# Tables 4 to 7 of the S5 mixer asked for at once by ScalarE, in memory of their own

## What is computed

```python
def s5_layer(u, a_re, a_im, b_re, b_im, c_re, c_im, d_skip, log_dt, w_glu):
    A_bar = jnp.exp(dt * A)                        # 64 groups, 64 complex states each
    bu = jnp.einsum('blgk,gpk->blgp', ug, B_bar)
    _, states = lax.associative_scan(combine, (a, bu), axis=1)
    y = jnp.einsum('gkp,blgp->blgk', C_mat, states).real.reshape(Bsz, L, Dm)
    y = jax.nn.gelu(y + d_skip.astype(f32) * uf).astype(u.dtype)
    y1, y2 = jnp.split(y @ w_glu, 2, axis=-1)
    return y1 * jax.nn.sigmoid(y2)
```

## Time and profile before

| | |
|---|---|
| median of 3 runs | 2110.14 us (2110.12 to 2112.23) |
| profiled execution, its own time | 2109.24 us |
| its span | 2106.9 us (2.3 us lie around it) |
| PE busy | 2045.2 us, 97% of the span |
| DVE, ACT, POOL busy | 1155.7, 603.3, 46.2 us |
| S5 mixer, blocks 0 to 7 | from 1573 to about 1660 us |
| granted TensorE clock, mean | 0.992 of full |
| DMA | 314.90 MB, SyncE's queue (q1) 287.32, ScalarE's (q10) 26.48 |

### The profile page before, as it was taken

The page is one execution under the profiler, slowest core; times in us unless marked ns, Lnnn a source line. Parts: engine busy times, 40 slices in busy tenths (PEclk is TensorE's granted clock), DMA queues, the critical chain, the costliest instruction groups (busy, mean ns, idle before and its releaser), DMA issues.

```text
span 2106.9 us, 26044 instructions
## 1 busy us (share of the span) xinstructions
PE 2045.2 (97%) x10332; PEld 1744.3 (83%) x10332; DVE 1155.7 (55%) x1653; ACT 603.3 (29%) x717; POOL 46.2 (2%) x55
## 2 busy tenths in 40 slices
PE   4999999999999999999999999999998999999998
PEld 3788888998898889888888988888877798888886
DVE  6677556655455436887444566644458564333322
ACT  2322221423323223222222323322231333222222
POOL 2000000000000000000000000000002000000000
PEclk9999999999999999999999999999999999999999
DMA  8455555433233143667544254544766423233221
GB/s 319 144 195 192 187 190 175 141 120 105 75 109 105 65 155 116 200 229 232 183 166 150 94 159 148 169 148 149 243 206 232 158 80 100 100 100 100 90 95 55
DMA packets 246575, 314.90 MB, mean 149 GB/s; under 512 B 31904, under 2 KB 219552, under 8 KB 244128
## 3 DMA queue, kind: packets, MB, share of 16 engines
q1 hardware_dynamic: 214160, 287.32, 41.4%
q10 hardware_dynamic: 32336, 26.48, 3.8%
HBM read 290.44 MB, written 27.53 MB: 151 GB/s over the span
## 4 chain that ended last, share of the span: by engine, by line
PE 76%; issue 15%; DVE 4%; DMA 3%; ACT 1%; POOL 0%; SPq 0%; ACTq 0%; POOLq 0%; DVEq 0%
PE ps L1779 18%; PE ps L1780 18%; PE ps L1781 18%; PE ps L1806 7%; PE ps L1807 7%; PE ps L1810 7%; DMA y_dram<-s_buf 1%; DVE ada_first L972 1%; DMA y_dram<-acc 1%; PE ps L2058 1%; DMA sq<-y_dram 1%; DMA csil<-in_c 0%; DVE w_lo L962 0%; PE ps L1901 0%; PE ps L2049 0%
## 5 line engine op out<-in xcount | busy, mean ns | idle before, releaser
L557 ACT ACTIVATE w_hi<-w_raw 128x1024 fp32r<-128x1024 f32 x352 | 345.9, 1029 | 353.7 <-PE ps L1781 241.1
L962 DVE TENSOR_TENSOR w_lo<-w_raw,w_hi 128x1024 fp32r<-128x1024 f32 x172 | 210.2, 1222 | 371.8 <-ACT w_hi L557 369.9
L1779 PE MATMUL ps<-g_hi,w_lo 128*128 128x512 f32 (+1 forms) x952 | 345.7, 363 | 0.0
L1781 PE MATMUL ps<-g_hi,w_hi 128*128 128x512 f32 (+1 forms) x952 | 344.9, 362 | 0.0
L1780 PE MATMUL ps<-g_lo,w_hi 128*128 128x512 f32 (+1 forms) x952 | 344.9, 362 | 0.0
L1779 PE MATMUL ps<-h_hi,w_lo 128*128 128x512 f32 x880 | 344.2, 391 | 0.3 <-DVE w_lo L962 0.3
L1781 PE MATMUL ps<-h_hi,w_hi 128*128 128x512 f32 x880 | 342.7, 389 | 0.0
L1780 PE MATMUL ps<-h_lo,w_hi 128*128 128x512 f32 x880 | 342.6, 389 | 0.0
L1806 PE MATMUL ps<-h_hi,w_lo 128*128 128x512 f32 x688 | 269.8, 392 | 2.3 <-DVE w_lo L962 2.0
L1807 PE MATMUL ps<-h_hi,w_hi 128*128 128x512 f32 x688 | 268.6, 390 | 0.0
L1810 PE MATMUL ps<-h_lo,w_hi 128*128 128x512 f32 x688 | 212.3, 390 | 0.0
(11 more groups left out here) (264 smaller groups left out, 2314.1 us busy)
## 6 DMA issues: line engine op xcount, KB each, us to landing
w_raw<-in_ffn_w_in SPq DMA_DIRECT2D x86, 1024.0 KB, 6.6
ada_raw<-in_ada_w SPq DMA_DIRECT2D x128, 512.0 KB, 4.6
w_raw<-in_ffn_w_out SPq DMA_DIRECT2D x32, 1024.0 KB, 6.5
w_raw<-in_ret_w_in SPq DMA_DIRECT2D x24, 1024.0 KB, 5.3
w_raw<-in_ffn_w_out SPq DMA_DIRECT2D x16, 768.0 KB, 4.5
tb<-s_rec SPq DMA_DIRECT2D x6, 1536.0 KB, 6.7
w_raw<-in_ret_w_out SPq DMA_DIRECT2D x8, 1024.0 KB, 5.1
w_raw<-in_s_w_glu SPq DMA_DIRECT2D x8, 1024.0 KB, 6.1
```

What stands on the lines that cost most here:

```text
L557: copy = lambda o, i: nc.scalar.activation(o, i, ACT.Copy)
L962: V.tensor_tensor(w_lo[k % 2][:, 0:HALF, :], w_raw[k % 2][:, 0:HALF, :], raw_f32(w_hi[k % 2][:, 0:HALF, :]), ALU.subtract).then_inc(w_lo_h ...
L1779: nc.tensor.matmul(o, wl, xh, start=start, stop=False)
L1781: return nc.tensor.matmul(o, wh, xh, start=False, stop=stop)
```

## The change

- ScalarE asks for tables 4 to 7, all eight DMAs, directly behind `gelu(0)`, after a wait until the last part of GLU weight pair 0 has been split. They go on ScalarE's DMA queue. They are no longer issued by SyncE, whose waits for them in the loop are gone.
- Table 6 lies over `w_raw[0]` and `w_raw[1]`, table 7 over table 0. Tables 4 and 5 stay where they were.
- GLU pair 1 is loaded into `w2_raw`, over table 2, is asked for behind the read of hop 3, with no wait on `w_lo_done`, and its split parts lie over tables 1 and 3.
- GLU pair 2, which goes into `w_raw`, waits for `outputs(6)`.

```diff
+        w_raw_at = place["end"]
         w_raw = [sb(f"w_raw{s}", [P, 8, CW]) for s in range(2)]
...
-        tables = [*tb, tb[2], tb[3]]
-        w2_hi, w2_lo = ([sb(f"w2_{part}{k}", [P, 8, CW], F32R, h_at + HB * k + 4 * 8 * CW * (part == "lo")) for k in range(2)]
-                        for part in ("hi", "lo"))
+        tables = [*tb, sb("tb6", [P, REC], F32, w_raw_at), tb[0]]
+        w2_raw = [sb(f"w2_raw{k}", [P, 8, CW], F32, g_at + 4 * 8 * CW * k) for k in range(2)]
+        w2_hi, w2_lo = ([sb(f"w2_{part}{k}", [P, 8, CW], F32R, (h_at, g_at)[k] + HB + 4 * 8 * CW * (part == "lo"))
+                         for k in range(2)] for part in ("hi", "lo"))
...
                 def glu_pair(dp):
+                    if dp == 2:
+                        sp.wait_ge(y_done, 7)
...
-                    if b + 4 < KT:
-                        sp.wait_ge(yt_in[b % 2], 16 * (b // 2 + 1))
-                        if b >= 2:
-                            sp.wait_ge(y_done, b + 1)
-                        table(b + 4)
-                    if b == 4:
-                        glu_pair(1)
+                    if b == 3:
+                        for k in range(2):
+                            sp.dma_start(w2_raw[k][:], glu_w[:, :, CW + (D, 0)[k]:2 * CW + (D, 0)[k]]).then_inc(w_landed[k], 16)
...
-                    copy(w2_hi[k][:, 0:HALF, :], w_raw[k][:, 0:HALF, :]).then_inc(w_hi_half, 1)
-                    copy(w2_hi[k][:, HALF:8, :], w_raw[k][:, HALF:8, :]).then_inc(w_hi_done, 1)
+                    copy(w2_hi[k][:, 0:HALF, :], w2_raw[k][:, 0:HALF, :]).then_inc(w_hi_half, 1)
+                    copy(w2_hi[k][:, HALF:8, :], w2_raw[k][:, HALF:8, :]).then_inc(w_hi_done, 1)
...
                     A(gy[b % 2], ps[:, 4 + 2 * (b % 2)], ACT.Gelu_apprx_tanh).then_inc(gelu_done, 1)
+                    if b == 0:
+                        act.wait_ge(w_lo_done, C_GLU + 3)
+                        for later in range(4, KT):
+                            act.dma_start(tables[later][:, 0:R_MT], rec[later]).then_inc(tb_in[later], 16)
+                            act.dma_start(tables[later][:, R_MT:REC], lag_rec[later]).then_inc(tb_in[later], 16)
...
-                    V.tensor_tensor(w2_lo[k][:, r, :], w_raw[k][:, r, :], raw_f32(w2_hi[k][:, r, :]),
+                    V.tensor_tensor(w2_lo[k][:, r, :], w2_raw[k][:, r, :], raw_f32(w2_hi[k][:, r, :]),
```

## The result

| | before | after |
|---|---|---|
| median | 2110.01 us (2108.33 to 2112.23, 12 runs) | 2112.71 us (2110.07 to 2114.11, 12 runs) |
| ratio to before | | 1.0015, 95% interval 1.0008 to 1.0022 |
| profiled execution, its own time | 2109.24 us | 2113.4 us |
| its span | 2106.9 us | 2110.9 us |

What follows compares the result with a forecast made beforehand. TensorE bounds the kernel, with mixer waits on transfers worth at most 9.4 us. Scan 3, 11.9 us late, less 9.4 gives +2.5: 2111.7 against the profiled 2109.24, plus 0.9 for the median, 2112.6; 8-in-10 range 2102.5 to 2117.

Steps and rivals of the forecast that it cites:

- The page's places to look: S5 mixer, 1620 to 1635 us: PE and DVE partly idle, waiting for late hop transfers and tables.
- the gain ceiling's terms: Mixer with free transfers: 7.70 us between scans 3 and 7 plus 1.66 of PE waits, together 9.4 at most.
- Equal counts of packets: DMA engines shared by ScalarE's and SyncE's queues: turns equal in packets, not bytes, so hop 0's read lands with the tables.
- The first rival: Hop 0's read slips through the tables unhindered, scan 3 on time: -9.4 us, 2100.7; chance 0.21.
- T: Landing time of hop 0's read in the mixer: about 1612.5 us, bounds 1609 to 1616.5.
- The range's low end: Lower end, 2102.5 us, of the 8-in-10 range for the kernel's time, reaching into the first rival's nearer half.
- the rival that decides below 385: Slower: same wait for hop 0's read, table stream slower; at 360 GB/s shift +6, 2116.1 us; chance 0.19.
- Write 0 at 0.6: Hop 0's write, 0.26 MB travelling among the tables, priced at 0.6 us at 412 GB/s.
- The path behind T: Mixer after hop 0's read lands: scan 3 starts at T + 1.4 = 1613.9, 11.9 us late; from there nothing late.
- The clock term: PE idle about 3.0 us before `outputs(7)`, possible lower clock: cost 0 to +2.5 us, taken at 0.
- the mark: Start of `first_glu(6)` on PE, 1655.59 us before; its shift is taken as the shift of the kernel's end.
- the prediction's sum: Shift of the mark: (T + 1.4 - 1601.95) - 9.4 = T - 1610, that is +2.5 us.

Runs made afterwards that it cites:

- the spaced-out variant: Changed kernel, but ScalarE asks for one table behind each of the first four GELUs, not all four behind the first: 2107.78 us, ratio 0.9991.

## Why the prediction was right

- **The page's places to look** held. All that moved lies in the mixer, and the gain ceiling's terms came back nearly to the digit: 7.7 us on DVE between scans 3 and 7, and both of PE's small waits gone.
- **Equal counts of packets** held, at 48 to 1 more sharply than in the earlier trace rows. This term decided the case. But not "in each microsecond from 1592 to 1610": in the first 2.9 us after the read's request there were 107 to none, from 1598 to 1599 63 to 14, and from 1594 to 1595, as the write ran out, 95 to 30. The first rival falls: read 0 landed at 1613.43, where a T below 1605.8 was needed. The range's low end, 2102.5, was taken from a read that gets through in a few turns of several packets each. No run shows such turns; in their place stand single packets, 17 to 17 and 3 to 3 in quarters of a microsecond. The landing time would not tell the two apart, since with equal batches on both queues 64 packets of the read meet 64 of the tables all the same, and counts over one or three microseconds do so only in part.
- **T = 1612.5**: measured 1613.45 - 0.68 = 1612.8. All queues together moved 410 GB/s from 1590 to 1605, where I had taken 412 from the earlier trace rows; the rival that decides below 385 had no footing.
- **Write 0 at 0.6** was mis-sized: 7.7 us, 5.7 more than the 2.0 before. Its packets are few (8 on each engine, 128 in all), but they went in turns with table packets (from 1592 to 1593 there were 31 of them beside 30 of 12 KB), and until 1590, 2.4 us after the request, none had been sent at all while 37 table packets went. By the trace's packets its first starts 3.2 us after the request, the last ends 4.0 later, where 8 turns of 0.47 are 3.8, and the landing comes 0.5 after that: the 7.7. It cost nothing here, since the read that follows still had to stay until the stream ended. In the spaced-out variant the same error was what I missed by.
- **The path behind T** held: scan 3 at 1614.84 - 0.68 = 1614.2 (1613.9 said), scan 7 at 1646.2 (near 1646), input blocks 6 and 7 landed 14.7 after their requests at 1598.3, so near 1613, and nobody waited for them. Hop 4's write, allowed 8.6 us behind pair 1, took 4.1.
- **The clock term, taken at 0 of 0 to 2.5**, was the wrong end. The idleness before `outputs(7)` was foreseen at 3.0 and was 2.78, and the group then took 3.50. No run shows the upper end, a cost of 2.5: against 2.00 the group lost nothing to 1.67 us in the runs (3.67 at a granted clock of 0.50 was the longest). The same 2.5 stands in the slower rival. The sum with it: T - 1610 = 2.8, plus 1.5 makes 4.3, and the mark moved by 3.96. So the prediction's sum, +2.5, was 1.5 us short of its own profile, and that the median came out at 2112.7 owes this much to the luck of the spread: in the medians after is 2.7 us slower, in the profiled executions 4.2.

Of the signs named ahead, read of hop 0 some 20 us (18.1), ScalarE idle about 14 (14.59), DVE about 12 (12.35), scan 7 near 1646 (1646.2) came. `first_glu(6)`, said near 1658, stood at 1659.55, by the clock term, and the equal counts came only once the small transfer had begun. One sentence on waits was too wide: "no idle above 0.3 before the later ones" holds for hops 1 to 5, but `output_lo(6)` waits 2.83 us, behind the long `outputs(7)`.

What I got wrong more than once was in the variants. In three of them (pair 1 a hop early, SyncE's wait taken out, two tables in front) I priced the read well, and the *next write* on the same queue too low or not at all: it meets whatever bulk was asked for ahead of it. SyncE's wait looked like the fault of the kernel before; taking it out gave 3.9 of the 9.4, and moving the table ahead of the read 8.0.

## What to carry to other kernels

Where a small transfer of many short packets has to be on time, don't put a bulk stream with long rows on the other queue beside it: each short packet paid for a long one here (68 of 256 bytes beside 67 of 12 KB from 1601 to 1603). My estimate from these runs, as long as the bulk lasts, is its own packets per engine times the time of one bulk packet (0.47 us for 12 KB, 0.16 for 4 KB), and some 3 us ahead of that (3.2 for write 0, 3.5 and 3.7 for the reads). Put the bulk on the same queue, in a place where the small one's chain waits anyway (here between the hop's write and its read, which made the kernel 8.0 us faster than before), and check what then lies ahead of the *next* small transfer. If it must be the other queue, cut the bulk's rows: a third of the packet took 3.1 us off the write (7.7 to 4.6) and 2.9 off the read (18.1 to 15.2).

## What I had not expected of the hardware

- A transfer that joined a bulk stream on the other queue sent nothing for a while: read 0 for 3.5 us beside 12-KB packets (107 of them, 1.2 MB, went ahead of it in the first 2.9) and for 3.7 beside 4-KB ones (395, 1.4 MB, in 3.4), against 1.0 to the first packet of a read alone. The bytes ahead are about the same, the packets are not. A write of 8 packets per engine, with 3.2 us to its first packet, took 7.7 us where it took 2.0 alone, and as much beside one table as beside four. What makes the pause, the traces do not show.
- Equal turns were not seen in every stretch. In the variant with 4-KB rows, from 1590 to 1591 us, write 0 sent 120 packets beside 58 of the tables'. Why it got ahead there stays open; the read that followed went by equal counts.
- A queue drained unevenly: with all four tables on one queue, one engine ran on for 2.5 us after the stream, at 16 to 33 GB/s where all together moved some 400, and a small write behind them took 18.45 us.
- `outputs(7)` after about the same idleness took 3.50 to 3.67 us in four kernels (2.78, 2.91, 2.92 and 2.80 us idle; granted clock 0.50 to 0.55), 2.75 in one (2.89 idle, 0.69) and 2.00 in another (2.59 idle, 1.00). Each is one execution. The windows without a mix of the two show a granted clock of 0.50 or of 1.00, and which of them PE got after a gap of this length differed between kernels, so a term for it belongs in the range, and not at zero where the gap is known.
